# Sample streams' query-times-state products: from eight full-width matmul pairs to four 32-column array tiles, streams in another order

## The reference, cut to what matters

```
o_x   = einsum('bhnd,bhdv->bhnv', qc * q_decay, S)      # the 16 queries times the state
o     = scores @ v + o_x
S_new = S * chunk_decay + einsum('bhmd,bhmv->bhdv', kc * k_decay, vc)
```

## Time and profile before

| | |
|---|---|
| time, median of 3 | 2603.92 us (2603.88 to 2604.22) |
| profiled execution: span from its first to its last instruction | 2601.3 us |
| PE (matmul) busy | 2559.3 us, 98% |
| PEld (weight load) busy | 2118.4 us, 81% |
| DVE busy | 925.9 us, 36% |
| ACT busy | 679.9 us, 26% |
| POOL busy | 219.5 us, 8% |
| moved by DMA | 265.28 MB, mean 102 GB/s |

### The profile page before, as it was taken

How to read it: one execution, slowest core, us unless ns; L and a number is a source line. 1 busy time by engine, 2 the same in 40 slices (tenths; PEclk the granted TensorE clock), 3 DMA queues, 4 the chain that set the end, 5 groups by cost and what they waited for, 6 DMA issues and landing times.

```text
span 2601.3 us, 33463 instructions
## 1 busy us (share of the span) xinstructions
PE 2559.3 (98%) x11857; PEld 2118.4 (81%) x11857; DVE 925.9 (36%) x1483; ACT 679.9 (26%) x1058; POOL 219.5 (8%) x301
## 2 busy tenths in 40 slices
PE   8999999999999999999999999999999999999997
PEld 6888888888887888888888878888888878888885
DVE  3333333333335322433433333333333352234334
ACT  4221121121123212522452122121112232225124
POOL 1101001002001000000010010010010010000003
PEclk9999999999999999999999999999999999999998
DMA  7343233234233222122332332332332432222223
GB/s 246 97 114 123 68 100 128 68 98 139 68 97 124 93 101 101 66 81 81 126 107 76 113 123 67 114 122 66 115 114 69 120 103 98 94 101 77 97 69 113
DMA packets 177678, 265.28 MB, mean 102 GB/s; under 512 B 15768, under 2 KB 122032, under 8 KB 177536
## 3 DMA queue, kind: packets, MB, share of 16 engines
q1 hardware_dynamic: 143968, 174.89, 20.7%
q0 software_dynamic: 23280, 75.71, 8.7%
q10 hardware_dynamic: 10288, 12.70, 2.1%
HBM read 221.24 MB, written 42.00 MB: 101 GB/s over the span
## 4 chain that ended last, share of the span: by engine, by line
PE 98%; DVE 1%; issue 1%; ACT 0%; DMA 0%; ACTq 0%; POOL 0%; POOLq 0%; DVEq 0%
PE acc L1126 28%; PE acc L1128 28%; PE acc L1127 28%; PE side L1162 9%; PE osb L1162 2%; PE side L1158 2%; PE side L1217 1%; DMA stage<-in_g_ple 0%; ACT stage L506 0%; ACT H L704 0%; DVE H L898 0%; ACT Z L501 0%; PE side L1358 0%; DVE Z L1072 0%; ACTq L128 0%
## 5 line engine op out<-in xcount | busy, mean ns | idle before, releaser
L1126 PE MATMUL acc<-Whi,Ahi 128*128 128x512 f32 x3200 | 1276.0, 399 | 8.7 <-issue 5.5
L1128 PE MATMUL acc<-Whi,Alo 128*128 128x512 f32 x3200 | 1248.0, 390 | 0.0
L1127 PE MATMUL acc<-Wlo,Ahi 128*128 128x512 f32 x3200 | 1247.2, 390 | 0.0
L451 ACT ACTIVATE Whi<-raw 128x1024 fp32r<-128x1024 f32 x321 | 340.3, 1060 | 1511.1 <-PE acc L1128 1508.1
L1126 PEld LDWEIGHTS acc<-Whi,Ahi 128*128 128x128 f32 x3200 | 601.5, 188 | 141.5 <-issue 9.1
L1128 PEld LDWEIGHTS acc<-Whi,Alo 128*128 128x128 f32 x3200 | 600.9, 188 | 127.5
L1127 PEld LDWEIGHTS acc<-Wlo,Ahi 128*128 128x128 f32 x3200 | 601.9, 188 | 117.5
L732 DVE TENSOR_TENSOR Wlo<-raw,Whi 128x1024 fp32r<-128x1024 f32 x321 | 396.0, 1234 | 718.4 <-ACT Whi L451 715.9
L742 DVE SCALAR_TENSOR_TENSOR Alo<-side,parl,Ahi 128x512 fp32r<-128x512 f32 (+1 forms) x198 | 98.3, 544 | 137.7 <-ACT Ahi L459 107.6
L357 POOL DMA_DIRECT2D out_new_ret_sample<-Ss x64 | 47.2, 738 | 820.2 <-DVE Ss L881 817.5
L1013 DVE COPY Z<-side 128x512 f32<-128x512 f32 (+1 forms) x48 | 28.9, 603 | 229.9 <-PE side L1162 229.9
(11 more groups left out here) (108 smaller groups left out, 1178.8 us busy)
## 6 DMA issues: line engine op xcount, KB each, us to landing
raw<-in_w_in SPq DMA_DIRECT2D x386, 256.0 KB, 2.8
raw<-in_w_out SPq DMA_DIRECT2D x128, 256.0 KB, 3.3
raw<-in_w_pg SPq DMA_DIRECT2D x128, 256.0 KB, 3.2
Ss<-in_state_ret POOLq DMA_DIRECT2D x64, 256.0 KB, 6.0
out_new_ret_sample<-Ss POOLq DMA_DIRECT2D x64, 256.0 KB, 2.8
h_residual<-H POOLq DMA_DIRECT2D x8, 1280.0 KB, 13.3
Z<-h_residual POOLq DMA_DIRECT2D x8, 1280.0 KB, 8.0
X<-kv_parts ACTq DMA_DIRECT2D x16, 384.0 KB, 5.4
```

Source lines behind the costliest of these rows:

```text
L451: nc.scalar.activation(Whi[:, p % 2], raw[:, p % 2], ACT.Copy).then_inc(w_hi, 1)
L1126: nc.tensor.matmul(acc[:, t], Ahi[:, k, tok], Whi[:, p % 2, kk], start=(s == 0), stop=False)
L1127: nc.tensor.matmul(acc[:, t], Ahi[:, k, tok], Wlo[:, p % 2, kk], start=False, stop=False)
L1128: mm = nc.tensor.matmul(acc[:, t], Alo[:, k, tok], Whi[:, p % 2, kk], start=False, stop=(s == KT - 1))
```

## The change

The four streams of one part go to four tiles of the array, each 32 columns wide. `qTm` now has a block of 32 columns (two streams' rows) for each stream: 16 columns hold the stream's queries, and the other 16 stay zero. A matmul loads 32 stationary columns, at the array columns `b // 2 * 32`, and writes only the 32 rows of `osb` with this number. In order that the four streams of a part fall on four different tiles, the streams are taken in the order 0, 4, 2, 6, 1, 5, 3, 7; state loads, stores and updates follow the same order. The loop over halves is now outside of the loop over streams. The number of matmuls, their contraction and the 256 moving columns stay as they are.

```diff
-SPREAD = [0]
-for _b in range(SB - 1):
-    SPREAD.append(SPREAD[_b] + max(P - SL * (_b + 1), SL * (_b + 1)))
-SPREAD_W = SPREAD[-1] + P
+STREAMS = (0, 4, 2, 6, 1, 5, 3, 7)
+BLOCK = 2 * SL
+SPREAD_W = 768
...
-                        po.dma_start(Ss[:, b % 4], st_v[one(l, 1), b, one(h, 1)]
+                        po.dma_start(Ss[:, b % 4], st_v[one(l, 1), STREAMS[b], one(h, 1)]
...
-                        po.dma_start(nst_v[one(l, 1), b, one(h, 1)].rearrange("l h p k c -> p (l h k) c"),
+                        po.dma_start(nst_v[one(l, 1), STREAMS[b], one(h, 1)].rearrange("l h p k c -> p (l h k) c"),
...
-                                qTm[:, half, SPREAD[b] + b * SL:SPREAD[b] + (b + 1) * SL],
+                                qTm[:, half, b * BLOCK + b % 2 * SL:b * BLOCK + b % 2 * SL + SL],
...
-                    def stream_output(b):
-                        pe.wait_ge(s_in[b % 4], hh * 32 + 16 * (b // 4 + 1))
+                    def stream_outputs(part):
+
                         for half in range(2):
-                            last = mm(osb[:, 0:DH], qTm[:, half, SPREAD[b]:SPREAD[b] + P], Ss[:, b % 4, half],
-                                      start=False, stop=(b == SB - 1 and half == 1))
-                        if b == SB - 1:
+                            for j in range(4):
+                                b = STREAMS[part * 4 + j]
+                                if half == 0:
+                                    pe.wait_ge(s_in[j], hh * 32 + 16 * (part + 1))
+                                rows = slice(b // 2 * BLOCK, (b // 2 + 1) * BLOCK)
+                                last = nc.tensor.matmul(osb[rows, 0:DH], qTm[:, half, b * BLOCK:(b + 1) * BLOCK],
+                                                        Ss[:, j, half], start=False, stop=(part == 1 and half == 1),
+                                                        tile_position=(0, b // 2 * BLOCK))
+                        if part == 1:
                             last.then_inc(os_ready, 1)
...
-                        block_rows = slice(b // 4 * STACK_BASE, b // 4 * STACK_BASE + STACK)
-                        kv = X[block_rows, b % 4]
+                        s = STREAMS[b]
+                        block_rows = slice(s // 4 * STACK_BASE, s // 4 * STACK_BASE + STACK)
+                        kv = X[block_rows, s % 4]
...
-                            for b in range(4):
-                                stream_output(b)
+                            stream_outputs(0)
...
-                            for b in range(4, 8):
-                                stream_output(b)
+                            stream_outputs(1)
```

## The result

| | before | after |
|---|---|---|
| time, median of 4 | 2604.07 us (2603.88 to 2604.89) | 2564.03 us (2563.42 to 2564.75) |
| ratio to before | | 0.9843, 95% interval 0.9831 to 0.9855 |
| span of the profiled execution | 2601.3 us | 2562.2 us |
| PE busy / PEld busy | 2559.3 / 2118.4 us | 2518.1 / 2070.6 us |

The forecast was 2586 us, 17.6 saved. 40.0 were saved: inside the range (2560 to 2608), the forecast way, but more than twice the size. The time lies outside the ordered queue's own range (2580 to 2597) and is near that of the four-way rival, 2567, for whose sake the whole range went so low.

A forecast was written before the change was run, and what follows sets the result against it. PE's queue of matmuls, busy 98% of the span, was taken as the bound. From 2603.9 us, -20.8 (overlap of tiles) + 3.5 (mode changes) - 0.3 (updates) = -17.6 gave 2586.3 us; range 2560 to 2608.

The forecast's parts named there:

- ordered queue: Query products: matmuls start strictly in order, 9 slots a part instead of 16, 20.8 us saved over 16 parts; 50%.
- four-way rival: Query products: each tile has its own queue, a part takes 0.95 us, 40.0 us saved, 2567 us in all; 27%.
- PE is the bound: Whole kernel: PE is busy 98% of the span, nothing else comes late, so all of the saving reaches the end.
- Changes of mode: Ways in and out of tiles around both parts of each head: 0.44 us a head, 3.5 us added for 8.
- Loads of 32 columns: Tiled query products: a weight load of 0.03 us that isn't hidden, estimated as a quarter of 0.11 for 128 columns.
- Update pairs: State updates at steps 8, 9, 14: neighbours on different rows overlap, 0.3 us saved in all, ends 0 and 2.8.

The follow-up runs named there:

- e1: Changed kernel with the loop over halves inside the loop over streams, so a stream's four records stand together on one tile; 2565.20 us.
- e9: e5 with all eight records of one tile ahead of the other tile's eight in each part; 2592.57 us.
- e2: Changed kernel with all four streams of the first part on the same tile, the second part as in the change; 2585.14 us.
- e5: Changed kernel with two tiles of 64 columns instead of four of 32, the streams alternating between them; 2578.80 us.
- e6: Changed kernel with the first part's tiled matmuls moved from step 7 to step 8, directly ahead of the updates of two streams; 2561.88 us.
- e3: Changed kernel with stream order 0,2,4,6,1,3,5,7, so neighbouring updates share their block of rows again; 2568.32 us.

## Why the prediction was wrong, point by point

- **PE is the bound, and all that is saved in its queue reaches the end: right, but for one place.** No state load or weight came late; the waits that grew are start-up (0.6), "issue" (1.0) and one for VectorE (0.5). The exception is the last update pair of a head. In head 0 it saves 0.23, and 0.17 of it is lost 5 us later: PE's first big matmul of the next group starts 216.91 - 216.46 = 0.45 us behind the one ahead of it, where it was 220.97 - 220.69 = 0.28. Just there ScalarE, which empties `acc`, waits for VectorE to free `stage` (after: 2.02 us of idle at 216.17; before: 1.82).

```profile
216.17 1.29 ACT L505 ACTIVATE stage<-acc,rstd 128x512 f32<-128x512 f32 x2 [2.02 <-DVE H L958]
```

- **"An ordered queue, 9 slots a part, 1.30 us saved": wrong, and this is the failed step.** I took it that the second record of a stream, waiting for its own tile, holds back the next stream. e1 shows that it doesn't, with up to three of a tile waiting. A part takes 4 rounds, 0.88 us; it saves 3.45 - 0.88 = 2.57, and 16 parts 41.1 us instead of 20.8. The four-way rival had 40.0, at 27%; its three loads of 0.03 a part are what the part didn't cost. e9 shows that the idea wasn't baseless: with eight in a row the queue does hold.
- The Trainium skill ("TensorE: Matmul & The Clock Gate", Part 2, What happens when you issue a matmul), on which I leaned in that choice, says that matmuls stay in program order. The runs disagree for matmuls on different tiles: by that rule e1 has 13 slots a part, and it has 4. The measurement decides.
- **Changes of mode, 0.44 us a head: right.** The drain of 0.09 is in the start of the first tile record. The first part takes 1.20, of which 0.88 is 4 rounds (in the traces e2's and e5's differences give 0.21 and 0.22 a round) and 0.32 the ways in and out, as forecast. e6's trace has 0.51 for three changes.
- **Loads of 32 columns, 0.03 each: the size is borne out where it shows**, at the part's start (0.12 in, with the drain). It doesn't show as a load that starts 0.03 ahead, as I had said (PEld's and PE's rows both start at 176.00), but as a first record of 403 ns instead of 379. As a term of each stream it was void: the loads of the other tiles run beside the matmuls.
- **Update pairs, 0.3 us in all, 2.8 at most: mis-sized.** I let one of the four matmuls overlap, less its load; in fact the loads of both blocks of rows also run side by side (0.30 us instead of 0.53), and a pair of two updates takes as long as one update alone, 0.43 to the next group (181.06 - 180.63; one alone in the earlier trace rows), 0.23 less. Two pairs a head in full and a quarter of the third are 8 x 0.51 = 4.1 us (e3: 4.3). It lies beyond my upper end, which was worked out with the same ordered queue.
- **The sum by the runs' terms:** -41.1 + 3.5 - 4.1 = -41.7; measured -40.0, and -39.1 between the spans of the two profiled executions. Of the 2.6 us between -41.7 and -39.1, 1.6 are the longer start-up and "issue" waits; there is one such execution of each kernel, so whether they belong to the change is not shown.

## What to carry to other kernels

Where TensorE is the bound and a product uses 32 of 128 stationary columns, or 48 of 128 rows, put such matmuls on different tiles next to each other: a group costs the records of its fullest tile, plus 0.32 us for the ways in and out. The order within the group mattered little with four records of one tile in a row; eight in a row cost four slots, and nothing between was tried. Put groups with different tilings side by side, and pair up small matmuls on different rows: each change of mode that this saves was worth about 0.2 us here, nearly a record's slot of 0.216.

## What the runs showed of the hardware that was not expected

- Matmuls of different tiles start out of the order of the queue: four at once within 0.15 us, though each fp32 matmul is two records on one tile, and with four records of a tile in a row as well (1.09 against 1.07 us for the part).
- That has a limit: with eight in a row, the other tile started only 0.92 us later, with three of the first tile still waiting.
- Neighbours on rows 0 to 47 and 64 to 111 run fully side by side, weight loads of 128 columns too: 0.23 us less for a pair whose four matmuls and loads took 0.47.
- Four moving operands of 128 rows, read at once, cost a matmul nothing: a round is 0.22 us with one tile busy (e2, 3.64 us for 16) or four (0.88 us for 16).
